# Delta levels 1 to 5: the transposed inverse by products, X from it by TensorE's transposition and ScalarE's copy

## The reference, cut to what matters

```python
kk = jnp.einsum("bhncd,bhnjd->bhncj", k, k)
m = jnp.where(strict, beta[..., :, None] * kk * decay, 0.0) + jnp.eye(C, dtype=f32)
rhs = jnp.concatenate([v * beta[..., None], k * (beta * jnp.exp(gc))[..., None]], axis=-1)
sol = lax.linalg.triangular_solve(m, rhs, left_side=True, lower=True, unit_diagonal=True)
u0, w = sol[..., :dv], sol[..., dv:]
```

## Time and profile before

| what | us |
|---|---|
| median of three timed runs | 3426.75 (3426.71 to 3431.73) |
| the profiled execution, its own time | 3424.14 |
| its span | 3422.4 |
| PE busy | 3297.6 (96%) |
| PEld busy | 2767.2 (81%) |
| POOL busy | 1707.1 (50%) |
| DVE busy | 1545.6 (45%) |
| ACT busy | 864.0 (25%) |

### The profile page before, as it was taken

How to read it: one execution, slowest core, us unless ns; L and a number is a source line. 1 busy time by engine, 2 the same in 40 slices (tenths; PEclk the granted TensorE clock), 3 DMA queues, 4 the chain that set the end, 5 groups by cost and what they waited for, 6 DMA issues and landing times.

```text
span 3422.4 us, 47301 instructions
## 1 busy us (share of the span) xinstructions
PE 3297.6 (96%) x17232; PEld 2767.2 (81%) x17232; DVE 1545.6 (45%) x2049; ACT 864.0 (25%) x1291; POOL 1707.1 (50%) x1748
## 2 busy tenths in 40 slices
PE   8999999999999999999999999999998999999996
PEld 7877888888888888888788887787777878778685
DVE  6722245444544454445441314343355565631723
ACT  5411133322332233223320102111113333310411
POOL 0255634433433353335326777766665555556684
PEclk9999999999999999999999999999999999999998
DMA  6322212111221122112224223322223222223222
GB/s 237 125 86 91 93 44 79 68 55 55 74 74 55 55 74 74 55 55 86 89 73 171 91 98 135 105 81 91 98 101 115 74 87 70 93 93 123 76 97 86
DMA packets 53530, 306.52 MB, mean 90 GB/s; under 512 B 5044, under 2 KB 7220, under 8 KB 21716
## 3 DMA queue, kind: packets, MB, share of 16 engines
q1 hardware_dynamic: 34528, 248.53, 21.0%
q10 hardware_dynamic: 18932, 57.00, 4.4%
HBM read 284.74 MB, written 20.77 MB: 89 GB/s over the span
## 4 chain that ended last, share of the span: by engine, by line
PE 83%; DVE 11%; ACT 3%; issue 2%; DMA 1%; ACTq 0%; DVEq 0%
PE gemm_ps L410 19%; PE gemm_ps L412 19%; PE gemm_ps L411 19%; DVE arena L849 8%; PE bankC L557 4%; PE bankB L555 3%; PE bankA L545 3%; PE gemm_ps L766 2%; DVE a_lo L849 2%; PE gemm_ps L768 2%; PE gemm_ps L767 2%; ACT arena L1549 2%; PE bankA L722 2%; DVE arena L855 1%; ACT a_hi L1549 1%
## 5 line engine op out<-in xcount | busy, mean ns | idle before, releaser
L410 PE MATMUL gemm_ps<-a_hi,w_hi 128*128 128x512 f32 (+1 forms) x3472 | 1383.5, 398 | 14.9 <-DVE a_lo L849 13.5
L386 POOL CAST w_hi<-w_raw 128x512 fp32r<-128x512 f32 x872 | 549.3, 672 | 1668.5 <-issue 1508.4
L412 PE MATMUL gemm_ps<-a_hi,w_lo 128*128 128x512 f32 (+1 forms) x3472 | 1330.3, 383 | 0.0
L411 PE MATMUL gemm_ps<-a_lo,w_hi 128*128 128x512 f32 (+1 forms) x3472 | 1328.5, 383 | 0.0
L378 POOL TENSOR_TENSOR w_lo<-w_raw,w_hi 128x512 fp32r<-128x512 f32 x872 | 1161.6, 1363 | 4.2
L410 PEld LDWEIGHTS gemm_ps<-a_hi,w_hi 128*128 128x128 f32 x3472 | 656.3, 189 | 147.9 <-DVE a_lo L849 16.3
L412 PEld LDWEIGHTS gemm_ps<-a_hi,w_lo 128*128 128x128 f32 x3472 | 654.6, 189 | 130.1
L411 PEld LDWEIGHTS gemm_ps<-a_lo,w_hi 128*128 128x128 f32 x3472 | 656.5, 189 | 121.4 <-issue 8.7
L849 DVE TENSOR_TENSOR arena<-gemm_ps,arena 128x512 f32<-128x512 f32 (+3 forms) x161 | 107.1, 665 | 613.8 <-PE gemm_ps L412 494.0
L849 DVE RECIPROCAL arena<-arena 128x512 f32<-128x512 f32 (+2 forms) x70 | 172.8, 2468 | 322.0 <-ACT arena L1549 320.0
L1549 ACT ACTIVATE arena<-arena 128x512 f32<-128x512 f32 (+5 forms) x350 | 214.6, 613 | 392.8 <-DVE arena L849 377.8
(11 more groups left out here) (162 smaller groups left out, 2692.0 us busy)
## 6 DMA issues: line engine op xcount, KB each, us to landing
w_raw<-w_stream SPq DMA_DIRECT2D x236, 1024.0 KB, 4.8
y_scratch<-arena ACTq DMA_DIRECT2D x20, 512.0 KB, 3.5
arena<-y_scratch ACTq DMA_DIRECT2D x13, 512.0 KB, 4.2
arena<-gc_scratch ACTq DMA_DIRECT2D x12, 512.0 KB, 3.7
arena<-x_t ACTq DMA_DIRECT2D x2, 2048.0 KB, 10.0
arena<-y_scratch ACTq DMA_DIRECT2D x1, 4096.0 KB, 25.4
x_scratch<-arena ACTq DMA_DIRECT2D x1, 4096.0 KB, 15.9
y_out<-arena ACTq DMA_DIRECT2D x4, 1024.0 KB, 3.9
```

The lines of the kernel that those rows point to most:

```text
L386: pool.tensor_copy(part(w_hi, w, q), part(w_raw, w, q)).then_inc(pool_step, 1)
L410: pe.matmul(o, hi, a_hi[:, k, 0:width], start=(k == 0), stop=False)
L411: pe.matmul(o, hi, a_lo[:, k, 0:width], start=False, stop=False)
L412: last = pe.matmul(o, lo, a_hi[:, k, 0:width], start=False, stop=(k == KT - 1))
```

## The change

In levels 1 to 5 "whole" makes only the product for `XT` (`bankC`), and VectorE only updates `XT`. A new step "turn" for each head transposes the four matrices of `XT` with TensorE into `bankB`, and ScalarE copies all of `bankB`'s half to `X`. "half" of the next level waits for that copy (now counted in `t1_sbuf`) in place of `lvl`. Level 6 is as before. The written order of a level is half 0, half 1, whole 0, whole 1, one block, turn 0, one block, turn 1, one block. There are as many blocks in a level as before, three, and as many by the beginning of level 6.

```diff
 DN_STEPS = ([("natural", 10), ("values", 8), ("transposed", 6)]
-            + [(s, l, a, w) for l in range(1, LEVELS)
-               for s, a, w in (("half", 0, 2), ("half", 1, 0), ("whole", 0, 1), ("whole", 1, 0))]
+            + [(s, l, a, w) for l in range(1, LEVELS - 1)
+               for s, a, w in (("half", 0, 0), ("half", 1, 0), ("whole", 0, 0), ("whole", 1, 1), ("turn", 0, 1),
+                               ("turn", 1, 1))]
+            + [(s, LEVELS - 1, a, w) for s, a, w in (("half", 0, 2), ("half", 1, 0), ("whole", 0, 1), ("whole", 1, 0))]
             + [("solved", 6)]
...
+        def product_count(j, l, a):
+
+            return (4 * (LEVELS - 2) + 2) * j + 4 * (l - 1) + a + 1
...
                     if l > 1:
-                        pe.wait_ge(s["lvl"], level_count(j, l - 1, a))
+                        pe.wait_ge(s["t1_sbuf"], product_count(j, l - 1, a) + 2)
...
                 elif step[0] == "whole":
                     l, a = step[1:3]
-                    pe.wait_ge(s["t1_sbuf"], level_count(j, l, a))
+                    pe.wait_ge(s["t1_sbuf"], product_count(j, l, a))
                     if l == 1:
                         pe.wait_ge(s["kd_ready"], j + 1)
                     for n in range(NB):
-                        if l < LEVELS - 1:
-                            pe.matmul(quad(bankB)[:, a, n, :], XT[:, a, n, :], T1[:, a, n, :],
-                                      start=True, stop=True)
                         last = pe.matmul(quad(bankC)[:, a, n, :], T1[:, a, n, :], XT[:, a, n, :],
                                          start=True, stop=True)
+                    last.then_inc(s["dd"], 1)
+                elif step[0] == "turn":
+                    l, a = step[1:3]
+                    pe.wait_ge(s["lvl"], level_count(j, l, a))
+                    for n in range(NB):
+                        last = pe.transpose(quad(bankB)[:, a, n, :], XT[:, a, n, :], ident)
                     last.then_inc(s["dd"], 1)
...
-                    v.wait_ge(s["dd"], level_count(j, l, a))
-                    if l < LEVELS - 1:
-                        copy_after(v.copy_predicated, X[:, a, :, :], low[:, l:l + 1, :].to_broadcast([P, NB, P]),
-                                   quad(bankB)[:, a, :, :])
+                    v.wait_ge(s["dd"], product_count(j, l, a))
...
-                    op(T1[:, a, :, :], quad(bankA)[:, a, :, :], ACT.Copy, s["t1_sbuf"], level_count(j, l, a))
+                    op(T1[:, a, :, :], quad(bankA)[:, a, :, :], ACT.Copy, s["t1_sbuf"], product_count(j, l, a))
+                elif step[0] == "turn":
+                    l, a = step[1:3]
+                    act.wait_ge(s["dd"], product_count(j, l, a) + 2)
+                    op(X[:, a, :, :], quad(bankB)[:, a, :, :], ACT.Copy, s["t1_sbuf"], product_count(j, l, a) + 2)
...
-DN_VECTOR_STEPS = 48
+DN_VECTOR_STEPS = 38
```

## The result

The changed kernel takes 3438.03 us (median of 13 runs, 3433.96 to 3439.70) where the kernel before takes 3427.57 us (13 runs, 3425.89 to 3431.73) beside it. The ratio is 1.0027 with a 95% interval of 1.0020 to 1.0035: slower by 7 to 12 us. The forecast was 3421.8 us, and the range ended at 3433. The sign is wrong. The mean granted clock is 0.985 or 0.986 in every one of the 13 runs of the kernel after, where the runs of the kernel before that stand beside the experiments have 0.989 to 0.991; 0.5% of 3430 us is 17 us, and that much more was lost at half clock in the timed runs too, not in the profiled one alone.

A forecast was written before the change was run, and what follows sets the result against it. The prediction took TensorE's (PE's) stream to bound the kernel. Eleven trips at -1.0 us and the last pair's -4.1 gave -15.1 us; +10.2 us for half clock left -4.9, so 3421.8 us, range 3409 to 3433.

The forecast's parts named there:

- What bounds the kernel: PE, busy in 96% of the span; an edit counts by PE work removed and waits opened there.
- a level's cost: A steady level takes 7.44 us on PE: 5.34 us for 48 records, 2.10 us for three large-product blocks.
- a transposition's price: One PE record of 0.11 us, half a product; a turn 0.44 us against 0.89 us for four products.
- Cover of the turns and of their copies: Blocks and products in each level hide ScalarE's copies and VectorE's XT update, by 0.37 us; turns stall nothing.
- Waits 2 and 3: PE before whole 0: on kd_ready at level 1, +1.39 us a trip; on tile 1's silu at level 4, +1.76 us.
- Wait 3: Level 4: tile 1's silu, queued on ScalarE ahead of the T1 copy, makes whole 0 wait, +1.76 us a trip.
- The sum of a trip: PE's removed and added work plus three waits: -1.0 us a trip, -11.0 us in 11 trips.
- The clock: Level 1's 2.42 us gap brings half clock one time in two: six spells at 1.7 us, +10.2 us.
- The last pair: The pair without taps, silu or wait on kd_ready: -4.1 us.
- the second, "the clock falls for longer, in every trip": Rival: level 1's gap costs 3.4 us of half clock in all 11 trips, +22 us, 3449 us; chance 0.13.
- the short price: Within the second rival: 1.7 us for each spell after level 1's gap, +4 us in total.

The follow-up runs named there:

- turn_twice: The kernel after with each turn's four transpositions done twice, the same result: 3485.77 us, ratio 1.0156 to the kernel before.
- products_gap: The kernel before with only the two blocks between half 0 and half 1 of level 1 moved behind whole 0: 3451.43 us, ratio 1.0051.
- kd_late: The kernel after without TensorE's own wait on kd_ready at level 1: 3403.42 us, ratio 0.9917 to the kernel before.
- silu_late: The kernel after with ScalarE's silu of tile 1 moved behind its T1 copy of half 1 of level 4: 3402.97 us, ratio 0.9920.
- products_pad: products_gap with four products done twice in half 0 of level 5, making a trip 0.89 us longer: 3464.94 us, ratio 1.0100.
- order_only: The kernel before, all products and both predicated copies kept, in the change's written order with turns doing nothing: 3497.23 us, ratio 1.0197.

## Why the prediction was wrong

Two steps failed: the number of spells at half clock, and, with a smaller share, the sum of a trip. The waits and the prices of the work were right.

**What bounds the kernel, a level's cost, a transposition's price:** right. In every experiment the time followed what the edit took off PE's stream or put onto it, up to the half clock. A level fell by 0.77 us where the terms give 0.89 - 0.06 - 0.02 = 0.81; turn_twice gives 0.11 us for a transposition. The row that the prediction reads for the step "transposed" (L528) is that of the step "values"; both are eight transpositions, and the price is the same. The Trainium skill ("TensorE: Matmul & The Clock Gate", Terms) calls the transposing mode "4× faster for FP32". Read as four times a product's speed, that makes 24 us for the doubling as an estimate; it cost 48 us, so the trace disagrees.

**Cover of the turns and of their copies:** right. No row of waits names a turn in the kernel after.

**Waits 2 and 3:** right in place, releaser and idle time: 2.40 us against 2.42 at level 1, 3.40 against 3.2 in the first trip, 1.75 against 1.76 at level 4. Each stood in PE's stream in full; taking them away gave their length back. Wait 3 cost somewhat more than its idle row: "whole" 0 begins 1290.84 - 1287.15 = 3.69 us after half 0, not 1.78 us, 1.91 us. ScalarE's copy of tile 1 came 0.09 us later (0.29 us behind the end of the tile on PE, not 0.20), behind the copy for turn 0, and VectorE began its taps at 1287.12, 0.12 us after it and not 0.03.

**The sum of a trip:** the first term that failed, and the one that took the time out of the range. I had -1.0 us. A trip without half clock was 114.13 us after 114.66, -0.53 us. From the timeline: level 1 +0.47, levels 2, 3 and 5 -0.76 each, level 4 (1287.15 to 1295.71, 8.56 us) +1.12: -0.69; the rest, +0.2, lies at the end of level 6, where VectorE starts its last copy 1.42 us after the products and not 1.23, and PE waits 0.26 us before "solved". The prediction held that nothing changes from level 6 on. The largest slips, at levels 4 and 6, are 0.2 us each; with 0.05 us in each of levels 2, 3 and 5 they make 0.5 us a trip, 5 us in 11.

**The clock:** the step that decided the sign. The mechanism and its price held: a gap of 2.4 us can bring half clock for 3.4 us, 115.77 - 114.13 = 1.64 us lost. The number did not: "with one in two I expect six spells in 11 trips". It was 10 and 9 in two profiles. One in two came from eight single gaps, each at its own moment. The eleven gaps here are no eleven lots: they follow one another at one distance, the half clock begins a little later with each, and the kernel after gave 10 and 9, others 10, 9, 5, 4 or none. Over the seven profiles with gaps of 2.4 us at level 1 it is 47 of 77, not far from the one half; I had the mean roughly and took its spread for that of independent events. Four spells more are 6.6 us, and they alone turn the forecast's -4.9 us into +1.9 us.

**The account:** -4.9 forecast, +5 for the trip's sum, +7 for the spells make +7, between the 10.5 us of the first session and the 4.4 us of the last. The range, 3409 to 3433 us, was wide enough for every number of spells at the forecast's own sum of a trip: 3412 us with none, 3429 with ten, 3430 with eleven. Only with the 5 us of the trips' sum do ten spells reach its edge, 3434 us; the 4 us from there to the measured 3438 are the rest that is spoken of below. From the first whole of level 1 in the first trip to that in the eleventh the profile shows 1614.63 - 458.60 = 1156.0 us where before has 1606.32 - 459.77 = 1146.6, +9.5: ten trips at -0.53 and nine spells within them at 1.64. The last pair gave its part back as foreseen, about 4 us: the record of the large product that starts at 2105.89 us before starts at 2113.64 us after, 7.75 us later, near the +7 of the account. The profiled execution is a further 5 us longer behind the delta heads, where it has other gaps and spells (a gap of 2.53 us at 2158 us with a spell, which the profile of before has not); the timed ratio, 7 to 12 us, is the better measure of the change. That gap is no sign of the exchange: products_gap, which has no exchange, shows it, and kd_late and silu_late, which have it, do not. Why it comes in some profiles, and whether a part of the tail is systematic, stays open.

**The rivals:** the second, "the clock falls for longer, in every trip", named the right side and the right place, with 3.4 us each and 3449 us; the truth was the short price with almost every trip, for which the rival's text had +4 us and little weight. The transpositions behind the gap as its reason fell with kd_late and products_pad.

## What to carry to other kernels

When a step is halved, look at what it covered: here the products' own time and two blocks hid a wait for VectorE and one queued behind a silu, and the new written order opened both, for 66 us of cost against 62 of gain. Of a wait kept from the old code it should be asked again what it protects (`kd_ready` guarded a bank that "whole" no longer writes), and taking away that one line and moving one silu turned +0.3% into -1.5%. An idle gap of TensorE of 2.1 to 2.4 us costs its own length here and, at 2.4 us, in somewhat over half of the cases 1.7 us of half clock. In a loop the trips don't draw that chance one by one: the length of a trip ties the answers together (nearly all in the kernel after, every second in products_pad from the fourth trip on, every fourth in silu_late, none in products_gap), so the range must hold none and all, and the slips of the other terms beside them. And one time that lands in a range shows nothing until its profile shows the mechanism (products_gap).

## What the runs showed that I had not expected

- The same gap of 2.4 us was followed by half clock in 10, 9, 10, 9, 5, 4 and 0 of 11 trips in seven kernels or executions. 0.89 us more in a trip, far from the gap, moved it from 0 to 5. No run varied the length of a trip by itself beyond that.
- 2.08 us of idle time were enough for a spell at level 4 of order_only, in 6 of 11 trips; the gaps of 1.75 us in the kernel after (22 in two profiles) and in kd_late (11), and those of 1.03 us in the kernel before, brought none.
- The kernel before itself runs between 3425.9 and 3435.3 us over the sessions. A part of it is of this kind too: its profile has five spells between 448 and 2131 us, of 3.4 to 6.8 us each.
